# Modulation groups 4 to 11 of a two-block transformer kernel: weighted sums on GpSimd instead of TensorE

## What is computed

```python
mod = jax.nn.silu(c) @ w_mod[l] + b_mod[l]                      # 1024 -> 6144
sh_m, sc_m, gt_m, sh_f, sc_f, gt_f = [m[:, None, :] for m in jnp.split(mod, N_MOD, axis=-1)]

h = rms_norm(x, g_mix_norm[l]) * (1.0 + sc_m) + sh_m
proj = h @ w_in[l]              # q_a k_a v_a q_i k_i w_i q_b k_b v_b gate_a gate_b
...
o_a = dsa_attention(q_a, k_a, v_a, q_i, k_i, w_i)               # 64 best keys of an index score
o_b = moba_attention(q_b, k_b, v_b)
merged = (jax.nn.sigmoid(gate_a) * (o_a @ w_br_dsa[l])
          + jax.nn.sigmoid(gate_b) * (o_b @ w_br_moba[l]))
x = x + gt_m * (merged @ w_out[l])

h = rms_norm(x, g_ffn_norm[l]) * (1.0 + sc_f) + sh_f
g_ff, u_ff = jnp.split(h @ w_gate_up[l], 2, axis=-1)
x = x + gt_f * ((jax.nn.silu(g_ff) * u_ff) @ w_down[l])
```

## Time and profile before

| | |
|---|---|
| median of 3 runs | 1503.77 us (1503.14 to 1507.26) |
| profiled execution, span from first to last instruction | 1501.4 us |
| PE busy | 1458.0 us, 97% |
| DVE busy | 850.9 us, 57% |
| ACT busy | 689.9 us, 46% |
| POOL busy | 36.2 us, 2% |
| TensorE's mean granted clock | 0.995 of full speed |
| transferred | 270 MB, 180 GB/s on average |

### The profile page before, as it was taken

How to read it: one execution, slowest core, us unless ns; L and a number is a source line. 1 busy time by engine, 2 the same in 40 slices (tenths; PEclk the granted TensorE clock), 3 DMA queues, 4 the chain that set the end, 5 groups by cost and what they waited for, 6 DMA issues and landing times.

```text
span 1501.4 us, 18041 instructions
## 1 busy us (share of the span) xinstructions
PE 1458.0 (97%) x6944; PEld 1164.5 (78%) x6944; DVE 850.9 (57%) x1032; ACT 689.9 (46%) x875; POOL 36.2 (2%) x53
## 2 busy tenths in 40 slices
PE   6999999999999999999999999999999988999998
PEld 3657686788888888888888888788888865788887
DVE  2677765654556545556754545466455667655443
ACT  2444453444344443454454344654434675554432
POOL 0010100000000000000000000100000020000000
PEclk9999999999999999999999999999999999999999
DMA  9763845565554655546556565555655530356561
GB/s 335 275 211 112 280 169 175 173 212 190 176 194 140 224 191 175 194 142 223 173 185 190 182 196 177 167 170 192 192 176 193 185 101 1 113 170 194 184 192 73
DMA packets 187880, 270.11 MB, mean 180 GB/s; under 512 B 8350, under 2 KB 134118, under 8 KB 187816
## 3 DMA queue, kind: packets, MB, share of 16 engines
q1 hardware_dynamic: 186448, 267.01, 54.3%
q10 hardware_dynamic: 1208, 1.94, 0.5%
q0 software_dynamic: 160, 0.26, 0.2%
HBM read 268.15 MB, written 1.05 MB: 179 GB/s over the span
## 4 chain that ended last, share of the span: by engine, by line
PE 87%; DVE 5%; ACT 3%; DMA 2%; issue 2%; SPq 0%; POOL 0%; DVEq 0%; ACTq 0%
PE bank L1772 26%; PE bank L1774 26%; PE bank L1773 26%; PE bank L1802 2%; DVE w_lo_ring L1284 2%; ACT w_hi_ring L940 1%; PE bank L1910 1%; PE bank L1939 1%; PE bank L2090 1%; DMA raw_ring<-in_w_out_dram 1%; DMA raw_ring<-in_w_in_dram 1%; DMA arena<-in_w_mod_dram 1%; PE bank L1993 1%; PE bank L1922 0%; PE bank L2069 0%
## 5 line engine op out<-in xcount | busy, mean ns | idle before, releaser
L1284 DVE TENSOR_TENSOR w_lo_ring<-raw_ring,w_hi_ring 128x2048 fp32r<-128x2048 f32 (+1 forms) x228 | 518.3, 2277 | 412.3 <-ACT w_hi_ring L1227 329.6
L1772 PE MATMUL bank<-w_hi_ring,h_hi 128*128 128x512 f32 x1360 | 543.4, 400 | 5.1 <-issue 1.8
L1774 PE MATMUL bank<-w_hi_ring,h_lo 128*128 128x512 f32 x1360 | 531.4, 391 | 0.0
L1773 PE MATMUL bank<-w_lo_ring,h_hi 128*128 128x512 f32 x1360 | 530.7, 390 | 0.0
L1227 ACT ACTIVATE w_hi_ring<-raw_ring 128x2048 fp32r<-128x2048 f32 x158 | 302.6, 1915 | 295.5 <-PE bank L1774 292.2
L1772 PEld LDWEIGHTS bank<-w_hi_ring,h_hi 128*128 128x128 f32 x1360 | 255.8, 188 | 73.2 <-issue 22.3
L1774 PEld LDWEIGHTS bank<-w_hi_ring,h_lo 128*128 128x128 f32 x1360 | 255.7, 188 | 55.1
L1773 PEld LDWEIGHTS bank<-w_lo_ring,h_hi 128*128 128x128 f32 x1360 | 256.2, 188 | 49.4
L1772 PE MATMUL bank<-w_hi_ring,f_hi 128*128 128x512 f32 (+1 forms) x456 | 177.0, 388 | 0.0
L1774 PE MATMUL bank<-w_hi_ring,f_lo 128*128 128x512 f32 (+1 forms) x456 | 176.0, 386 | 0.0
L1773 PE MATMUL bank<-w_lo_ring,f_hi 128*128 128x512 f32 (+1 forms) x456 | 175.7, 385 | 0.0
(11 more groups left out here) (257 smaller groups left out, 877.7 us busy)
## 6 DMA issues: line engine op xcount, KB each, us to landing
raw_ring<-in_ffn_w_gate_up_dram SPq DMA_DIRECT2D x176, 512.0 KB
raw_ring<-in_ffn_w_down_dram SPq DMA_DIRECT2D x44, 1024.0 KB
raw_ring<-in_w_in_dram SPq DMA_DIRECT2D x22, 1024.0 KB
raw_ring<-in_w_gate_up_dram SPq DMA_DIRECT2D x44, 512.0 KB
arena<-in_w_mod_dram SPq DMA_DIRECT2D x12, 1024.0 KB, 7.7
raw_ring<-in_w_mod_dram SPq DMA_DIRECT2D x12, 1024.0 KB
raw_ring<-in_w_down_dram SPq DMA_DIRECT2D x11, 1024.0 KB
raw_ring<-in_conv_w_in_dram SPq DMA_DIRECT2D x16, 512.0 KB
```

What stands on the lines that cost most here:

```text
L1284: dve.tensor_tensor(w_lo[:, u % RING, 0:words], raw[:, r % RING, 0:words], w_hi[:, u % RING, 0:words].bitcast(F32), ALU.subtract).then_inc ...
L1772: pe.matmul(dst, hi, whi, start=start, stop=False)
L1773: pe.matmul(dst, hi, wlo, start=False, stop=False)
L1774: return pe.matmul(dst, lo, whi, start=False, stop=stop)
```

## The change

Groups 0 to 3 stay as they are. For groups 4 to 11 the weighted sum over the eight blocks of 128 rows is made on POOL, in `acc`, as eight multiplications by a column of silu(c) (`c_col`, a new ACT instruction) and seven additions, each on 128x512, one after the other with a wait between. POOL issues the loads itself, four of 512 KB for each group, two in flight, into free parts of the arena (the region of gate b for groups 4 to 6; `qi_t` and `ro` for 7 to 11). PE then does one sum over partitions with a full table of ones (`ones`, in the memory of `c_act`). The loads of these groups leave SP's queue and `raw_ring`. The gate bias is loaded into all partitions of `gt` by a broadcast transfer from POOL, DVE adds the sum to it, and the bias product and `b_row` go. The sums move in the list: 4 behind vb, 5 behind ga, 6 behind ka's evacuation, 7 behind the first bb, 8 behind the first part of out1, 9 behind out1, 10 and 11 behind the body of the first feed-forward network. The hold in front of the second norm grows from 10 to 15, `mod_a` stands behind it.

```diff
-SIDE_MODS = (4, 5, 6)
-SIDE = 2
+POOL_MODS = range(4, 12)
...
-    part("qi", 0, 1, 2, [evac("qi"), mod(4, 0)])
-    part("ki", 0, 0, 1, [mod_row(4, 0), evac("ki"), mod(4, 1)])
-    part("qb", 0, 0, 2, [mod_row(4, 1), [dict(kind="kir")], mod(5, 0)], [[dict(kind="tp", stage="kiu", g=0)], []])
-    part("qb", 0, 1, 2, [mod_sum(4), tgroup("qi", 2), tgroup("ki", 1), mod_row(5, 0), evac("qb"), mod(5, 1)])
-    part("kb", 0, 0, 2, [mod_row(5, 1), mod(6, 0)])
-    part("kb", 0, 1, 2, [mod_sum(5), tgroup("qb", 2), mod_row(6, 0), evac("kb"), mod(6, 1)], [index[0], [], index[1], index[2]])
+    part("qi", 0, 1, 2, [evac("qi"), pool_mod(4)])
+    part("ki", 0, 0, 1, [evac("ki")])
+    part("qb", 0, 0, 2, [[dict(kind="kir")]], [[dict(kind="tp", stage="kiu", g=0)], []])
+    part("qb", 0, 1, 2, [tgroup("qi", 2), tgroup("ki", 1), evac("qb")])
+    part("kb", 0, 0, 2)
+    part("kb", 0, 1, 2, [tgroup("qb", 2), evac("kb"), [dict(kind="gt bias")], pool_mod(5), pool_mod(6)],
+         [index[0], [], index[1], index[2]])
...
-    part("vb", 0, 0, 2, [mod_row(6, 1)], [[], index[3], index[4], index[5] + rot[0]])
-    part("vb", 0, 1, 2, [mod_sum(6), evac("vb")], [rot[1], index[6], index[7], rot[2]])
+    part("vb", 0, 0, 2, [], [[], index[3], index[4], index[5] + rot[0]])
+    part("vb", 0, 1, 2, [evac("vb"), mod_sum(4)], [rot[1], index[6], index[7], rot[2]])
...
-    part("ga", 1, 1, 2, [evac("ga", 1), topk(0, 3), mod(7, 0)], inside[3])
-    part("qa", 0, 0, 2, [mod_row(7, 0), mod(7, 1), topk(1, 0)])
-    part("qa", 0, 1, 2, [mod_row(7, 1), evac("qa"), mod(8, 0)])
-    part("ka", 0, 0, 2, [mod_sum(7), mod_row(8, 0), mod(8, 1), topk(1, 1)])
-    part("ka", 0, 1, 2, [tgroup("qa", 2), mod_row(8, 1), evac("ka"), mod(9, 0)])
-    part("va", 0, 0, 2, [mod_sum(8), mod_row(9, 0), mod(9, 1), topk(1, 2), topk(1, 3)])
-    part("va", 0, 1, 2, [tgroup("ka", 2), mod_row(9, 1), evac("va")], held=True)
+    part("ga", 1, 1, 2, [evac("ga", 1), topk(0, 3), mod_sum(5)], inside[3])
+    part("qa", 0, 0, 2, [topk(1, 0)])
+    part("qa", 0, 1, 2, [evac("qa")])
+    part("ka", 0, 0, 2, [topk(1, 1)])
+    part("ka", 0, 1, 2, [tgroup("qa", 2), evac("ka"), mod_sum(6)])
+    plan.extend(pool_mod(7) + pool_mod(8) + pool_mod(9))
+    part("va", 0, 0, 2, [topk(1, 2), topk(1, 3)])
+    part("va", 0, 1, 2, [tgroup("ka", 2), evac("va")], held=True)
...
-    part("bb", 0, 0, 1, [mod(10, 0)])
-    part("ba", 0, 0, 1, [evac("bb", 0), mod_row(10, 0), mod(10, 1)])
-    part("bb", 1, 0, 1, [mod_sum(9), mod_row(10, 1), hold(7, 4), evac("ba", 0), evac("bb", 1), tgroup("merged", 4)[:2]])
-    add("mod_a", norm=1, half=0)
-    by_token_tile("ba", 1, 0, 1, behind=mod(11, 0))
-    part("out1", 0, 0, 2, [mod_row(11, 0), mod(11, 1)], [tgroup("merged", 4)[2:], mod_sum(10)])
-    part("out1", 0, 1, 2, [mod_row(11, 1), evac("out1", 0)])
+    part("bb", 0, 0, 1, [mod_sum(7)])
+    part("ba", 0, 0, 1, [evac("bb", 0)])
+    part("bb", 1, 0, 1, [hold(7, 4), evac("ba", 0), evac("bb", 1), tgroup("merged", 4)[:2]])
+    by_token_tile("ba", 1, 0, 1)
+    part("out1", 0, 0, 2, [mod_sum(8)], [tgroup("merged", 4)[2:], []])
+    part("out1", 0, 1, 2, [evac("out1", 0)])
     part("out1", 1, 0, 2)
     by_token_tile("out1", 1, 1, 2, last=True)
     add("square")
-    plan.extend(mod_sum(11) + hold(10, 4))
+    plan.extend(pool_mod(10) + pool_mod(11))
+    plan.extend(mod_sum(9) + hold(15, 4))
+    add("mod_a", norm=1, half=0)
     add("scale_x", norm=1)
...
-    ffn(0, "f0", 1, then=2)
+    ffn(0, "f0", 1, then=2, behind=mod_sum(10) + mod_sum(11))
...
+            loaded = [0, 0]
+
+            def load(m, q):
+
+                pool.dma_start(pool_in[m >= 7][q % 2], w_mod[:, 2 * q:2 * q + 2, 512 * m:512 * m + 512])\
+                    .then_inc(sem(f"pool_full{q % 2}"), 16)
+                loaded[q % 2] += 1
+
             for item in plan:
                 k = item["kind"]
+                if k == "gt bias":
+                    pool.wait_ge(sem("t_done"), find["tg", "mrow", (1, 3)] + 1)
+                    for i5, m in enumerate((2, 5)):
+                        pool.dma_start(gt[:, i5, :], A["b_mod"][0:1, m * D:(m + 1) * D].to_broadcast([P, D])).then_inc(sem("gt_bias"), 16)
+                if k == "pool mod":
+                    m = item["m"]
+                    a = acc[:, m % 2, :]
+                    if m == 4:
+                        pool.wait_ge(sem("t_done"), find["tg", "mrow", (1, 1)] + 1)
+                        pool.memset(ones, 1.0).then_inc(sem("ones_ready"), 1)
+                        pool.wait_ge(sem("c_ready"), 2)
+                    if m == 7:
+                        pool.wait_ge(sem("ix_done"), 8)
+                        pool.wait_ge(sem("t_done"), find["tg", "ka", 1] + 1)
+                    load(m, 0)
+                    load(m, 1)
+                    pool.wait_ge(sem("t_done"), find["tg", "sum", m - 2 if m >= 6 else (3, 1)[m - 4]] + 1)
+                    for q in range(4):
+                        pool.wait_ge(sem(f"pool_full{q % 2}"), 16 * loaded[q % 2])
+                        for kk in range(2):
+                            kt = 2 * q + kk
+                            w = pool_in[m >= 7][q % 2][:, kk, :]
+                            if kt == 0:
+                                tick.step(pool.tensor_scalar(a, w, c_col[:, 0:1], None, ALU.mult))
+                                continue
+                            tick.step(pool.tensor_scalar(w, w, c_col[:, kt:kt + 1], None, ALU.mult))
+                            ins = pool.tensor_tensor(a, a, w, ALU.add)
+                            if kt == KT - 1:
+                                ins.then_inc(sem("pool_sum"), 1)
+                            else:
+                                tick.step(ins)
+                        if q < 2:
+                            load(m, q + 2)
+                    pool.wait_ge(sem("pool_sum"), m - 3)
...
                     elif st in ("ga", "gb"):
+                        if st == "gb":
+                            act.wait_ge(sem("pool_sum"), 3)
...
-                    act.dma_start(b_row[0:1, :], A["b_mod"][0:1, 5 * D:6 * D]).then_inc(sem("b_row_full"), 16)
...
                         if which in (2, 5):
-                            dve.tensor_copy(gt[:, which // 3, 512 * (g % 2):512 * (g % 2) + 512], b[:, :]).then_inc(free, 1)
+                            gv = gt[:, which // 3, 512 * (g % 2):512 * (g % 2) + 512]
+                            dve.wait_ge(sem("gt_bias"), 16 * 2)
+                            dve.tensor_tensor(gv, b[:, :], gv, ALU.add).then_inc(free, 1)
```

58 lines of the change are left out of this document (27 added, 31 removed).

## The result

The changed kernel takes 1528.5 us (median of 5 runs, 1527.1 to 1535.7); the kernel before, timed beside it, 1507.2 us (5 runs). The ratio is 1.016 with a 95% interval of 1.013 to 1.019: it is 21 to 25 us slower, where 9.8 us of gain were forecast. The range ended at 1508. The profiled execution took 1535.7 us, the slowest of its five, with a span of 1533.9.

The account below looks back on a forecast made before the run. The prediction took the kernel as bound by PE, busy 97% of the span. PE's gain of 23.2 us, less 3.4 for late DVE and 10 for the shared port, gave 9.8: 1494.0 us as a median, range 1483 to 1508.

Parts of the forecast that it names:

- Net gain on PE, 23.2 us: On PE: 30.3 us of partial products, sums and bias work removed, less 6.4 for moved sums and 0.7 for holds.
- DVE late, 3.4 us: Stalls because DVE is late: 2.8 us at dsa's first softmax and 0.6 before kb's transposes, leaving 19.8 us of gain.
- the 2.8 us at the dsa softmax: PE stall at the first softmax of the dsa branch, which would lag gb's start by 6.7 us, not 3.3.
- PE's wait in front of kb's transposes: Behind kb's evacuation the transposes already wait 1.44 us for DVE; this was to grow by 0.6.
- The price of a bias product: Each of four bias products on PE takes 1.12 us in its row, 1.05 without overlap with its successor.
- 0, at most 0.3: Cost in us of the extra activation, b_row's loads and the broadcast load, said to lie beside other work.
- GpSimd's own time, 23 us a group: Eight scalings at 0.65 us, seven additions at 1.2, gaps between operations, and about 8 us for loads.
- rival C: GpSimd late with sum 9: each us above 28.9 a group costs PE 3; slower, 1512 at 35; chance 0.16.
- The shared port, 10 us of 0 to 18: DVE held by GpSimd's operations at four places where PE follows DVE closely: bounds 0 and 18 us, 10 taken.
- B: Rival: DVE loses its turn at every GpSimd operation, cost 18 us or more, 1502 us, within noise; chance 0.13.
- The signs named beforehand: Trace signs: splits above 2.28 us only beside GpSimd, PE waiting over 10 us for sum 9, rotations at old steps.
- rival A: GpSimd's operations never hold DVE, rotations keep old steps beside its scalings: 1484 us; chance 0.21.

## Why the prediction was wrong, point by point

**Net gain on PE, 23.2 us, and DVE late, 3.4 us: right.** With loads alone the kernel is 18.5 us faster (shift 18.1 at 470 us) where their difference said 19.8. The shift of 19.95 at the last out1 product looks closer than it is: sums 10 and 11 and the longer hold come later, so the forecast's terms make 22.6 there. In that run the 2.8 us at the dsa softmax are there, and PE's wait in front of kb's transposes is 1.9 us, 2.0 by the forecast. The partial products' records are down from 192 to 64. The price of a bias product holds, but the broadcast loads are not "0, at most 0.3" wherever they are put.

**GpSimd's own time, 23 us a group: the step that failed first.** The addition was right (1.2 forecast, 1.28 measured). The scaling was priced at 0.65 by the memset's row and takes 1.57: the nearest row of the right size was of the wrong kind. 8 x 1.57 + 7 x 1.28 = 21.5 us of operations instead of 13.6, and 30 us a group with loads when undisturbed (the run with fills), where the limit of rival C was 28.9. By itself this step would not have sunk the forecast: fills of that length land at 1495.8 us, inside the range.

**The shared port, 10 us of 0 to 18: the step that put the time out of the range, mis-sized, and counted once where it acts twice.** It cost 32.7 us (real operations against fills). By 267 us the shift lost about 22 us (-19.1 with fills, +3.2 with the real operations), above the upper bound of 18; this holds DVE's side and the waits for the root of qa and for sum 6, which the port lengthens. GpSimd's side stretched groups 7 to 9 from 30 to 36.2 us (108.7 us from 190.5 to 299.2), and that set off rival C. By C's own rule each us above 28.9 costs 3: 7.3 x 3 = 22 us, and 23 were measured. That they agree is partly luck: the rule lets PE arrive with its whole saving, 86.6 us behind the start; PE came after 90.6 us and waited 18.2, and what followed, the slow clock above all, made up the rest. The mechanisms of B and C both came true, and the forecast gave them separate chances as if one excluded the other, though both hang on the same lock. The sum would have been 19.8 - 22 - 23 = -25 us; the run is 21 to 25 slower, and 28 behind at 470 us in the profiled execution.

**Two things that no step had.** The root of qa behind group 6 (DVE waits 6.7 us): the forecast looked at GpSimd's arithmetic and not at what stands in its queue behind it. And the clock: the sum-9 stall alone costs 3 to 4 us on top of its 18.2.

**The signs named beforehand** were the right ones to look at: splits above 2.28 us only while GpSimd runs (2393 ns to 420 us), a wait for sum 9 of more than 10 us (18.2). The rotations at old steps (rival A) are refuted by 1118 ns against 686.

## What to carry to other kernels

An idle engine is not a free one: price its operations by a row of the same kind, and then ask which engine it shares a port with. If they lock one another, the cost appears twice, in the busy engine's deadlines and in the helper's. Give the helper only work that nobody waits for, in a stretch where the busy engine has no deadline either (here three groups of eight), and look at every short instruction that already stands in its queue.

Replacing real operations by fills of equal length is a cheap test that parts "too slow" from "in the way".

## What the runs showed of the hardware

- On GpSimd a multiplication of 512 columns by one value per partition (1.57 us, by a constant 1.49 to 1.55) is slower than an addition of two tensors (1.28 us) and three times a fill (0.53 us).
- Fills on GpSimd neither hold DVE nor are held by it (527 to 530 ns beside DVE's splits, splits at 2290 ns). Additions are held and hold; scalings are held (up to 3.8 us), but lengthen DVE's 512-column pieces only from 689 to 720 ns, where additions make it 869 and both together 971: of DVE's operations with two SBUF sources, 12 of 14 that started in the first 0.6 us of a scaling were held, and none of 19 that started later.
- An operation of DVE with one source in PSUM is not held by GpSimd's arithmetic (680 ns beside it, 682 before); with both in SBUF it is (999 ns, 692 before).
- Behind an idle stretch of 18 us PE worked at clock 0.50, its lower level of 1.2 GHz, until 306 us, about 6 us; behind a busy one it kept 2.4 GHz.
